# The head of a fused two-block kernel: first modulation reordered, four weight pieces on TensorE, early splits, tables loaded at another place

## The reference

```python
mod = jax.nn.silu(c) @ w + b                       # c: 1024, w: 1024 x 3072
shift, scale, gate = jnp.split(mod, 3)
h = rmsnorm(x, norm_w) * (1 + scale) + shift       # 256 x 1024
proj = h @ hyb_w_in                                # first projection of the hybrid layer
```

## Time and profile before

| what | us |
|---|---|
| median of 3 runs | 2144.03 |
| lowest and highest | 2142.12, 2148.79 |
| time of the profiled execution | 2143.46 |
| its span in the profile | 2141.7 |
| TensorE busy | 2010.9 (94%) |
| VectorE busy | 1719.9 (80%) |
| ScalarE busy | 1321.8 (62%) |

### The profile page before, as it was taken

How to read it: one execution, slowest core, us unless ns; L and a number is a source line. 1 busy time by engine, 2 the same in 40 slices (tenths; PEclk the granted TensorE clock), 3 DMA queues, 4 the chain that set the end, 5 groups by cost and what they waited for, 6 DMA issues and landing times.

```text
span 2141.7 us, 28565 instructions
## 1 busy us (share of the span) xinstructions
PE 2010.9 (94%) x10396; PEld 1663.3 (78%) x10396; DVE 1719.9 (80%) x2425; ACT 1321.8 (62%) x1972; POOL 0.2 (0%) x4
## 2 busy tenths in 40 slices
PE   5998899998998899999999999999999998999997
PEld 4786799978887678888888878788887876777776
DVE  6688788767777488989989898998989987885764
ACT  3344444346565377878778787877778774544543
POOL 0000000000000000000000000000000000000000
PEclk9999999999999899999999999999999999999998
DMA  8845689836332188999999899998999994762630
GB/s 301 317 155 192 210 305 321 306 128 219 128 109 98 50 296 325 365 350 359 349 341 358 326 371 351 349 361 328 361 326 375 357 358 146 230 225 73 211 110 20
DMA packets 154212, 560.20 MB, mean 262 GB/s; under 512 B 17233, under 2 KB 17489, under 8 KB 153937
## 3 DMA queue, kind: packets, MB, share of 16 engines
q1 hardware_dynamic: 154064, 558.29, 72.2%
HBM read 557.18 MB, written 1.05 MB: 261 GB/s over the span
## 4 chain that ended last, share of the span: by engine, by line
PE 75%; DVE 14%; ACT 6%; issue 3%; DMA 2%; SPq 0%; DVEq 0%; ACTq 0%
PE ps L524 21%; PE ps L526 20%; PE ps L525 20%; PE ps L530 11%; DVE spl L513 6%; PE ps L534 3%; ACT sph L501 3%; DVE macc L571 1%; ACT arena L1978 1%; DMA ring<-in_moe_down 0%; DVE arena L2012 0%; DMA ring<-in_hyb_w_in 0%; ACT ps L745 0%; DVE arena L841 0%; DVE hL L739 0%
## 5 line engine op out<-in xcount | busy, mean ns | idle before, releaser
L513 DVE TENSOR_TENSOR spl<-ring,sph 128x1024 fp32r<-128x1024 f32 x906 | 1078.0, 1220 | 304.3 <-ACT sph L501 295.1
L501 ACT ACTIVATE sph<-ring 128x1024 fp32r<-128x1024 f32 x906 | 948.8, 1058 | 553.8 <-PE ps L526 437.3
L524 PE MATMUL ps<-sph,hH 128*128 128x512 f32 (+1 forms) x1296 | 519.2, 401 | 3.5 <-DVE hL L739 3.5
L526 PE MATMUL ps<-sph,hL 128*128 128x512 f32 (+1 forms) x1296 | 506.6, 391 | 0.0
L525 PE MATMUL ps<-spl,hH 128*128 128x512 f32 (+1 forms) x1296 | 505.4, 390 | 0.0
L524 PEld LDWEIGHTS ps<-sph,hH 128*128 128x128 f32 x1296 | 245.1, 189 | 53.4 <-issue 5.7
L526 PEld LDWEIGHTS ps<-sph,hL 128*128 128x128 f32 x1296 | 244.5, 189 | 52.3
L525 PEld LDWEIGHTS ps<-spl,hH 128*128 128x128 f32 x1296 | 245.0, 189 | 48.0 <-issue 1.0
L524 PE MATMUL ps<-sph,rH 128*128 128x512 f32 x664 | 271.3, 409 | 5.6 <-ACT arena L2891 1.7
L525 PE MATMUL ps<-spl,rH 128*128 128x512 f32 x664 | 261.9, 394 | 0.0
L526 PE MATMUL ps<-sph,rL 128*128 128x512 f32 x664 | 261.6, 394 | 0.0
(11 more groups left out here) (300 smaller groups left out, 1764.0 us busy)
## 6 DMA issues: line engine op xcount, KB each, us to landing
ring<-in_moe_gu SPq DMA_DIRECT2D x448, 512.0 KB, 5.3
ring<-in_moe_down SPq DMA_DIRECT2D x224, 512.0 KB, 5.4
ring<-in_mod SPq DMA_DIRECT2D x144, 512.0 KB, 4.7
ring<-in_w_in SPq DMA_DIRECT2D x64, 512.0 KB, 4.3
ring<-in_dense_gu SPq DMA_DIRECT2D x44, 512.0 KB, 5.3
ring<-in_ssm_w_in SPq DMA_DIRECT2D x40, 512.0 KB, 3.5
ring<-in_dense_down SPq DMA_DIRECT2D x22, 512.0 KB, 5.5
ring<-in_hyb_w_in SPq DMA_DIRECT2D x20, 512.0 KB, 5.9
```

Of the source, the lines that this page charges most:

```text
L501: a.activation(k.high[m % SPLITS][:, 0:w], raw[:, 0:w], ACT.Copy).then_inc(k.S.half_rounded, 1)
L513: v.tensor_tensor(k.low[m % SPLITS][:, 0:w], raw[:, 0:w], k.high[m % SPLITS][:, 0:w], ALU.subtract).then_inc(*k.tick(k.S.half_split, f"hal ...
L524: pe.matmul(out, a[0], b[0], start=start, stop=False, skip_group_check=True)
L526: return pe.matmul(out, a[1], b[0], start=False, stop=stop, skip_group_check=True)
```

## The change

The order of the first modulation's pieces becomes 0, 2, ... 14 (the shift) and then 1, 3, ... 15 (the scale). Pieces 4, 12, 5 and 11 aren't touched by VectorE: TensorE multiplies each by the column of silu(c) itself, in 8 products of one column with 128 x 128 of the weights, added up in a bank of their own (`direct_tensor`), and the ring's buffer is free when these are done. The sum over partitions is made in two halves (`first_sum_tensor`): the shift's 8 products once piece 14 is in, the scale's once piece 15 is in. VectorE adds bias and the direct products first. VectorE takes its first three steps ahead of the first norm's small operations.

TensorE's program between transposes and first projection is now: shift sum; 3 fills; piece 5; 3 fills; piece 11; 4 fills; scale sum; 8 fills; then the 5 fills that were there. Pieces 4 and 12 stand ahead of the transposes.

ScalarE splits halves 0 and 1, and VectorE half 0, before they wait for the modulation. The modulated tiles are made for the first half of the features (both token blocks) first, and the first projection waits for those alone; the second half of the features is awaited two weight halves later. The remaining tables' loads stand ahead of chunk 22 instead of 26.

```diff
--- before.py
+++ after.py
@@ -400,9 +400,11 @@
         self.back = []
         for i in range(6):
             steps, gates = [("step", i, r) for r in range(2 * KD)], [("gate", i, 2 * KD + r) for r in range(KD)]
-            late = [] if i == 0 else [("rest", i, r) for r in range(3)] if i == 4 else gates[0:3]
-            before = [("gates", i - 1, 0)] if i > 0 else []
-            self.back += steps[0:3] + before + steps[3:] + late + [("sum", i, 0)] + [g for g in gates if g not in late]
+            late = [("rest", i, r) for r in range(3)] if i == 4 else gates[0:3]
+            if i == 0:
+                self.back += steps[0::2] + [("shift", 0, 0)] + steps[1::2] + [("sum", 0, 0)] + gates
+                continue
+            self.back += steps[0:3] + [("gates", i - 1, 0)] + steps[3:] + late + [("sum", i, 0)] + [g for g in gates if g not in late]
         self.back += [("rest", 5, 0), ("rest", 5, 1), ("gates", 5, 0)]
         self.at = {}
         at = 0
@@ -472,7 +474,7 @@
     for c, (src, width, freed) in enumerate(k.stream.chunks):
         if c == RING:
             sp.dma_start(k.cst[:, 0:512], d["cst"][:, 0:512]).then_inc(S.tables_landed, 16)
-        if c == 2 * KD + 10:
+        if c == 2 * KD + RING:
             for dst, src_ in ((k.cst[:, 512:], d["cst"][:, 512:]), (k.small[:, :], d["small"]), (k.postok[:, :], d["pos"]),
                               (k.dtw[:, :, :], d["dtw"])):
                 sp.dma_start(dst, src_).then_inc(S.start_landed, 16)
@@ -545,6 +547,8 @@
 
 BACK_PAUSE = ("gate", 4, 2 * KD)
 
+DIRECT = (4, 12, 5, 11)
+
 
 def back_vector(v, k):
 
@@ -552,14 +556,18 @@
         return
     kind, i, r = k.stream.back[k.at_back["vector"]]
     k.at_back["vector"] += 1
-    if kind == "rest":
+    if kind in ("rest", "shift"):
         return
     S, tick, when = k.S, k.tick, k.when
     mod, bias = k.d["mod"][i], k.V[f"b{i}"]
     if kind in ("step", "gate"):
         k.stream.ask(("mod", i, r), mod[r], QUARTER, f"mod{i}.step{r}")
+        if i == 0 and r in DIRECT:
+            return
         sem, value, w = landed(k, ("mod", i, r))
         n, part, before = (r // 2, r % 2, r - 2) if kind == "step" else (r - 2 * KD, 2, r - 1)
+        if i == 0 and before in DIRECT:
+            before -= 2
         c = k.st[:, mod_col(i) + n:mod_col(i) + n + 1]
         m = k.macc[:, part * D:(part + 1) * D]
         v.wait_ge(sem, value)
@@ -572,6 +580,11 @@
     elif kind == "sum":
         bank = k.banks[k.bank_of.get(f"mod{i}.sum", 0)]
         m = k.mods[:, i, 8:16]
+        if i == 0:
+            v.wait_ge(*when(f"mod0.step{DIRECT[-1]}"))
+            v.tensor_tensor(k.mods[:, 0, 0:16], k.banks[k.bank_of.get("mod0.direct", 0)][:, 0:16], bias[:, 0:16], ALU.add).then_inc(*tick(S.mod_ready, "mod0.biased"))
+            v.wait_ge(*when("mod0.biased"))
+            bias = k.mods[:, 0, :]
         v.wait_ge(*when(f"mod{i}.sum"))
         v.tensor_tensor(k.mods[:, i, 0:16], bank[:, 0:16], bias[:, 0:16], ALU.add).then_inc(*tick(S.mod_ready, f"mod{i}.summed"))
         v.wait_ge(*when(f"mod{i}.summed"))
@@ -591,7 +604,12 @@
         return
     kind, i, r = k.stream.back[k.at_back["tensor"]]
     k.at_back["tensor"] += 1
+    if i == 0 and kind == "step" and r in DIRECT:
+        direct_tensor(pe, k, r)
     if kind in ("step", "gate", "rest"):
+        return
+    if i == 0 and kind in ("shift", "sum"):
+        first_sum_tensor(pe, k, kind)
         return
     lo, hi, steps = (0, 16, f"mod{i}.step15") if kind == "sum" else (16, 24, f"mod{i}.step23")
     bank = k.back_banks.borrow(pe, f"mod{i}.{kind}" if kind == "sum" else f"mod{i}.gates", f"mod{i}.summed" if kind == "sum" else f"mod{i}.gated")
@@ -599,6 +617,31 @@
     for j in range(lo, hi):
         last = mm(pe, bank[:, j:j + 128], k.macc[:, j * 128:(j + 1) * 128], k.C["ones"])
     last.then_inc(*k.tick(k.S.mod_summed, f"mod{i}.sum" if kind == "sum" else f"mod{i}.gates"))
+
+
+def direct_tensor(pe, k, r):
+
+    n, part = r // 2, r % 2
+    if r == DIRECT[0]:
+        k.banks_turn.hand(pe, 1, "mod0.direct", ("mod0.biased",))
+    bank = k.banks[k.bank_of["mod0.direct"]]
+    sem, value, w = landed(k, ("mod", 0, r))
+    pe.wait_ge(*k.when("c.silu"))
+    pe.wait_ge(sem, value)
+    same = [x for x in DIRECT if x % 2 == part]
+    for j in range(8):
+        last = mm(pe, bank[:, 8 * part + j:8 * part + j + 1], w[:, j * 128:(j + 1) * 128], k.st[:, 16 + n:17 + n], r == DIRECT[0] and j == 0, r == same[-1])
+    last.then_inc(*k.tick(k.S.mod_summed, f"mod0.step{r}"))
+
+
+def first_sum_tensor(pe, k, kind):
+    if kind == "shift":
+        k.banks_turn.hand(pe, 2, "mod0.sum", ("mod0.summed",))
+    bank = k.banks[k.bank_of["mod0.sum"]]
+    pe.wait_ge(*k.when("mod0.step14" if kind == "shift" else "mod0.step15"))
+    for j in range(*((0, 8) if kind == "shift" else (8, 16))):
+        last = mm(pe, bank[:, j:j + 128], k.macc[:, j * 128:(j + 1) * 128], k.C["ones"])
+    last.then_inc(*k.tick(k.S.mod_summed, "mod0.shift" if kind == "shift" else "mod0.sum"))
 
 
 def back_steps(e, k, name, n, limit=None):
@@ -657,6 +700,8 @@
     if i > 0:
         back_until(pe, k, "tensor", i, "sum")
         fill(pe, k, banks, NORM_FILL[i])
+    else:
+        back_steps(pe, k, "tensor", 8)
     for t in range(NT):
         pe.wait_ge(*k.when(f"n{i}.x{t}"))
         for h in range(2):
@@ -666,29 +711,52 @@
                 last = turn(pe, k, bank[:, j * 128:(j + 1) * 128], k.norm_space.xn[:, t, c * 128:(c + 1) * 128])
             last.then_inc(*k.tick(k.S.norm_turned, f"n{i}.turn{t}.{h}"))
     if i == 0:
-        pe.wait_ge(*k.when("mod0.step10"))
-        fill(pe, k, k.banks_turn, 5)
+        back_steps(pe, k, "tensor", 3)
+        fill(pe, k, k.banks_turn, 3)
+        back_steps(pe, k, "tensor", 1)
+        fill(pe, k, k.banks_turn, 3)
+        back_steps(pe, k, "tensor", 3)
+        fill(pe, k, k.banks_turn, 4)
         back_until(pe, k, "tensor", 0, "sum")
+        fill(pe, k, k.banks_turn, 8)
 
 
...
     a.wait_ge(*when(f"mod{i}.ready"))
...
+    if i == 0:
+        norm_fill_scalar(a, k, 0, 0, 0)
+        for t in range(NT):
+            norm_round_scalar(a, k, 0, t, 0)
+        norm_fill_scalar(a, k, 0, 1, 1)
+        for t in range(NT):
+            norm_round_scalar(a, k, 0, t, 1)
+        return
+    for t in range(NT):
+        norm_fill_scalar(a, k, i, t, 0)
         for h in range(2):
-            a.wait_ge(*when(f"n{i}.full{t}.{h}"))
-            a.activation(k.hH[:, 4 * h:4 * h + 4, rows], fulls[2 * t + h], ACT.Copy).then_inc(*tick(S.h_rounded, f"n{i}.high{t}.{h}"))
+            norm_round_scalar(a, k, i, t, h)
+
+
+def norm_fill_scalar(a, k, i, t, h):
...
+def norm_round_scalar(a, k, i, t, h):
...
 def first_norm_vector(v, k):
@@ -713,9 +781,12 @@
 def norm_vector(v, k, i, before):
 
     S, tick, when = k.S, k.tick, k.when
-    xn, fulls = k.norm_space.xn, k.norm_space.fulls
+    xn = k.norm_space.xn
     if i == 0:
+        back_steps(v, k, "vector", 4)
         first_norm_vector(v, k)
+        back_steps(v, k, "vector", 13)
+        split_vector(v, k, 0)
     back_until(v, k, "vector", i, "sum")
     for t in range(NT if i > 0 else 0):
         v2, y, t0 = (k.st[:, n + t:n + t + 1] for n in (34, 36, 38))
@@ -726,18 +797,35 @@
...
+    if i == 0:
+        norm_fill_vector(v, k, 0, 1, 0)
+        norm_fill_vector(v, k, 0, 0, 1)
+        for t in range(NT):
+            norm_low_vector(v, k, 0, t, 0)
+        split_vector(v, k, 1)
+        for t in range(NT):
+            norm_low_vector(v, k, 0, t, 1)
+        return
...
@@ -885,13 +973,14 @@
     items, linear, pairs, one = (k.banks_turn.only(*n) for n in ((0, 1, 2), (3,), (5, 6), (7,)))
     k.back_banks = linear
     fill(pe, k, items, 5)
-    for n in range(4):
-        pe.wait_ge(*when(f"n0.low{n // 2}.{n % 2}"))
     live = []
     for name, width in HYB_ITEMS:
         m = k.stream.at["hyb", name]
         outs = {}
         for q in range(4):
+            if name == "kv" and q % 2 == 0:
+                for t in range(NT):
+                    pe.wait_ge(*when(f"n0.low{t}.{q // 2}"))
             w = [x.rearrange("p (k n) -> p k n", k=2) for x in half(pe, k, m + q)]
             for n in range(4 if name in FEATURES else 2):
                 b = n // 2 if name in FEATURES else n
```

More of the change, by code:

```diff
@@ L668, in norm_tensor @@
     if i == 0:
-        pe.wait_ge(*k.when("mod0.step10"))
-        fill(pe, k, k.banks_turn, 5)
+        back_steps(pe, k, "tensor", 3)
[4 more added lines that the diff above has]
+        fill(pe, k, k.banks_turn, 4)
         back_until(pe, k, "tensor", 0, "sum")
+        fill(pe, k, k.banks_turn, 8)
 def norm_scalar(a, k, i):
-    S, tick, when = k.S, k.tick, k.when
-    fulls = k.norm_space.fulls
+    when = k.when
     if i == 0:
@@ L680, in norm_scalar @@
         root_scalar(a, k, f"n{i}.{t}", k.st[:, 38 + t:39 + t], k.st[:, 34 + t:35 + t])
+    if i == 0:
+        split_scalar(a, k, 1)
     a.wait_ge(*when(f"mod{i}.ready"))
-    for t in range(NT):
[L683 to L688, removed]
```

(44 more changed lines are left out.)

## The result

The changed kernel takes 2151.16 us in the median of 20 runs; the kernel before, on the same chips, 2144.44 (20 runs). The ratio of their times is 1.0025, 95% interval 1.0014 to 1.0036: by it 5.4 us longer, 3.0 to 7.7 (the two medians by themselves differ by 6.7). Forecast were 2.4 us more, inside a band of 0.3% to either side. The profiled execution took 2146.39 us, 2.9 more than that of the kernel before.

A forecast was written before the change was run, and what follows sets the result against it. TensorE's in-order program was taken to bound the head: first product at 53.7 against 43.44 us, partly regained by a removed wait and half clock, net +2.4 on 2143.46, so 2145.9 us. Range 2137 to 2152.5 us.

The forecast's parts named there:

- the 2145.9 of the sum: Whole kernel: profiled execution of 2143.46 us plus a net 2.4 us gives 2145.9 us.
- The bound: Head up to the scale sum: TensorE's own program ends last, at 42.6 us; VectorE's last step ends at 32 to 34.
- from 22 us on the loads set VectorE's pace: VectorE's accumulating steps before the change: paced by weight loads, 1.28 us each, so fewer VectorE steps alone gain nothing.
- the sign: Behind the scale sum: fills end after VectorE's remainder by 5 us or more; 6.4 us forecast.
- The Trainium skill's figure: One-column products of the four pieces: 25 ns each, 1.6 us together; the forecast used 0.21 and 0.11 us instead.
- What comes back: First product to kv copies: idle falls from 4.8 to 0.8 us, full clock saves 2.2 us, net +2.4 us.
- the 6.2 (4 idle, 2.2 clock): At VectorE's kv copies: TensorE's wait falls from 4.8 to 0.8 us and half clock worth 2.2 us goes.
- P - 51.3: Net change of the kernel's time, P being the first projection product's start; forecast P is 53.7 us, so +2.4 us.
- The low clock behind pieces 5 and 11: Rival: half clock from piece 5 through scale sum and first fills loses 7 us, giving 2152.9 us; chance 0.22.
- That TensorE isn't the pace: Rival in the head: cheap pieces and early full clock let loads decide, first product at 45.0, 2137.2 us; chance 0.10.
- More gain from early tables than one hole: Rival: loads freed in the next 40 us remove other waits too, giving 2136 to 2140 us; chance 0.06.

The follow-up runs named there:

- the warmed run: Changed kernel with 20 unread products of the parameters ahead of everything on TensorE, against the kernel before: ratio 1.0016, 1.0002 to 1.003.

## Why the prediction was right, and where it was off

**The range.** The measured 2151.16 us lie in the range of 2137 to 2152.5, but 5.3 above the 2145.9 of the sum, and the forecast loss of 2.4 us lies just below the measured interval of 3.0 to 7.7. The upper part of the range was there mostly for a clock that falls again, which didn't happen; that the time fell inside was luck in part. What follows takes the mechanism step by step.

**The bound.** That TensorE's own program, and no longer loads or VectorE, would set the scale sum was right: 39.13 for its start against VectorE's 32.36, and the run without pieces moved it forward. There it came only 5.5 us earlier, not the 10.2 that the pieces take from start to start, since the transposes began 2.1 us later than cst's landing at 14.63, and the shift sum and the wait ahead of it took 2.3 us more, the fills 0.3. The reading that from 22 us on the loads set VectorE's pace fits the profile that it was made from; in the runs without pieces it is VectorE, at 1.39 us a step. The forecast has no term for the steps' new order; in the changed kernel nothing was felt of it, since the sum came 6.8 us behind VectorE.

**The terms.**

| term of TensorE's program | forecast, us | measured, us |
|---|---|---|
| begins with cst's landing | 15.54 | 14.63 |
| pieces 4 and 12, half clock | 6.8 | 6.95 |
| transposes | 3.65 | 3.65 |
| shift sum | 2.6 | 2.1 |
| pieces 5 and 11, from start to the next fill's start | 3.6 | 1.70 + 1.70 = 3.4 |
| ten fills | 8.5 | 2.58 + 2.66 + 3.52 = 8.8 |
| end of the scale sum | 42.6 | 41.1 |
| 13 fills behind it | 11.1 | 11.3 |
| first product | 53.7 | 51.7 |
| VectorE's last step ends | 32 to 34 | 32.36 |
| tables' loads go out | about 39 | 37.1 |

Of the 1.5 us at the scale sum's end 0.9 is cst's landing. The first product's record overlaps about the last 0.5 us of the fills. These end 6.8 us behind the first two remainders and 4.4 behind the last two; 5 or more had been named as the sign. The Trainium skill's figure (TensorE: Matmul & The Clock Gate, Back-to-back issue gap), from which the forecast worked out an estimate of 1.6 us for all four pieces, isn't what these products with a fresh weight load each show: 0.10 us a record at best, 0.21 cold. The section calls its table the gap of an isolated product, and says of a stream of weight loads and products that both set the spacing; with that the 0.10 agrees.

**What comes back.** The idle time before the copies was put at 0.8 and is 0.9; the low clock of 60 to 67 us is gone, as forecast; the clock shows full from 26 us on past the copies, to 138. The tables' edit alone brought 4.7 us in median time (ratio 0.998), beside the 6.2 (4 idle, 2.2 clock) that the prediction had credited it with. By the second profile of the kernel before the credit is 3.5 - 0.9 = 2.6 idle and 1.7 clock, 4.3 us.

**The size.** By P - 51.3 and P = 51.7 the loss would be 0.4 us, and the profile has 1.0 at the same point (66.01 - 62.80 - 2.2); the time says 5.4, 3.0 to 7.7. The term that was off is the reference, as far as the profiles tell: 51.3 was read from one execution of the kernel before whose head was the longer of two. With its second profile (copies' end 61.3, low clock until 65.1, so 1.7 us saved) the same difference is 66.0 - 61.3 - 1.7 = 3.0 us, at the lower end of the measured interval. What is left between 1 to 3 us and 5.4 lies behind the head, where the two profiles of the kernel before differ by 6.6 us; whether it is spread or an effect of the change there wasn't shown.

**The rivals.** The low clock behind pieces 5 and 11 didn't happen in either profile of the changed kernel (fills 0.43 us a record throughout), though the mechanism is real: the warmed run shows the clock falling in pieces 4 and 12. That TensorE isn't the pace fell with the changed kernel's own rows; only with the pieces and some or all fills gone does the scale sum wait for VectorE (1.47 and 6.60 us). More gain from early tables than one hole: the tables' run shows none.

**What the change is made of.** At the first product the early splits and tile order bring 3.8 us; at the copies the tables' place brings about 3 to 4 and the clock behind them about 2. Against them stand the pieces, which cost 5.5 us at the sum, and the 8 fills, 6.1 to 6.2 behind the sum in the profiles (10.6 us from the sum's end to the first product, and 4.4 to 4.5 without them). In the time the pieces' cost is clear (0.998 against 1.0025), that of the fills isn't. The order of the pieces and the sum in two halves were never undone by themselves. The net is a loss because the two parts meant to relieve VectorE and to keep TensorE busy sit on TensorE's in-order program.

## What to carry to other kernels

Filling work is in order too: count it like any other instruction between the last input and the first product, and stop it where the input arrives; here each record too many put the first product off by 0.43 us, and with none at all the kernel was as fast as with thirteen fills. Before moving steps off a busy engine, ask what the engine that takes them over holds up in exchange: VectorE with 16 steps finished earlier than with 12, because TensorE came late to its pieces and kept the ring's buffers. When steps of one accumulator are put behind one another, look at their spacing. And take a saving at the head for a saving in time only when the time shows it: 6.3 us at the copies brought none here. Last, read a reference point from more than one profile when the difference sought is a few microseconds.

## What the runs showed of the hardware

The display of the granted clock can't be read before the trace's first change of it. In the run without fills it says 1.00 in 31 to 34 us and in 39 to 41 us:

```profile
31.00:34.00 3.00, 3.00 (x16) 3.00 (x15) 0.59 (x1) 0.21 (x1) 0.00 (x0) 1.00 1.03 412
39.00:41.00 2.00, 2.00 (x11) 2.00 (x11) 2.00 (x4) 2.00 (x4) 0.00 (x0) 1.00 0.82 248
```

But the sum's 16 records took 3.78 us there, where with fills they took 1.95, and a product of 256 columns took 0.41 us, and 0.28 from 42.2 on. That is the pace of half clock; the durations are to be trusted, as in rows 7.

Products of one column, each with its own 128 x 128 weights, run at 0.10 us a record at full clock and 0.21 at half, and in the warmed run the clock fell from 1.00 to 0.50 amid them. A stream of loads that has been held pays the way from issue to landing again: in the changed kernel chunk 8 was released at about 18.1 us (14.63 plus half of 6.95), and VectorE's next step found its data only at 21.99, having waited 3.62 us:

```profile
21.99 0.75 DVE L576 TENSOR_SCALAR macc<-ring,st 128x1024 f32<-128x1024 f32 x1 [3.62 <-DMA ring<-in_mod]
```
